# A 3-block transformer kernel: single-unit weight ring, rewritten first norm, respaced top-k, rotations and output-projection waits

## The reference

```python
def rmsnorm(x, g):
    xf = x.astype(jnp.float32)
    y = xf * lax.rsqrt(jnp.mean(jnp.square(xf), axis=-1, keepdims=True) + EPS)
    return (y * g.astype(jnp.float32)).astype(x.dtype)

# block 1, mixer: h = rmsnorm(x); p = h @ w_in, split into the parts of two branches
#  sparse attention: index scores per query block of 128, then
_, idx = lax.top_k(score, n_keep)          # n_keep = 128 keys a query
#  and softmax attention over those keys, 8 heads of 64
#  retention: 4 heads, q and k turned by rotary(), decay mask, group norm, silu gate
return jnp.concatenate([a_out, r_out], axis=-1) @ w_out   # "output projection"

# block 3, first branch: forget-gate attention ("fox")
c = jnp.cumsum(jax.nn.log_sigmoid(f_logit.astype(jnp.float32)), axis=1)
s = s + (ci[..., :, None] - c_t[..., None, :])            # row sums added to the logits
```

## Time and profile before

| what | value |
|---|---|
| median of 3 runs | 2392.09 us |
| the profiled execution's own time | 2387.57 us |
| its span | 2385.8 us |
| granted TensorE clock, mean | 0.999 |
| busy: PE, VectorE, ScalarE, GpSimd | 98%, 46%, 36%, 39% |
| DMA, mean | 87 GB/s |

### The profile page before, as it was taken

How to read it: one execution, slowest core, us unless ns; L and a number is a source line. 1 busy time by engine, 2 the same in 40 slices (tenths; PEclk the granted TensorE clock), 3 DMA queues, 4 the chain that set the end, 5 groups by cost and what they waited for, 6 DMA issues and landing times.

```text
span 2385.8 us, 37842 instructions
## 1 busy us (share of the span) xinstructions
PE 2348.3 (98%) x15316; PEld 2066.7 (87%) x15316; DVE 1103.0 (46%) x1676; ACT 854.6 (36%) x1320; POOL 919.2 (39%) x382
## 2 busy tenths in 40 slices
PE   7999999999999999999999999999999999999999
PEld 7898999999999999898988888767667888888887
DVE  4885353573442534555644435343473337422222
ACT  4334433332222334554322224454464333322222
POOL 4321223344444442123444444422224455444443
PEclk9999999999999999999999999999999999999999
DMA  5121222222222231111232222322213333323232
GB/s 179 66 72 37 73 65 87 89 88 93 87 103 88 88 107 59 54 54 54 89 105 88 90 104 89 107 72 71 71 54 106 106 106 106 106 88 105 88 106 88
DMA packets 33463, 208.12 MB, mean 87 GB/s; under 512 B 3754, under 2 KB 6420, under 8 KB 9284
## 3 DMA queue, kind: packets, MB, share of 16 engines
q1 hardware_dynamic: 29552, 202.00, 24.7%
q10 hardware_dynamic: 3796, 4.45, 0.6%
HBM read 204.24 MB, written 2.12 MB: 86 GB/s over the span
## 4 chain that ended last, share of the span: by engine, by line
issue 59%; POOL 24%; PE 16%; POOLq 1%; DMA 0%; ACT 0%; DVE 0%; SPq 0%; DVEq 0%; ACTq 0%
POOL wl L2574 24%; PE ps L393 14%; PE ps L346 1%; PE ps L328 1%; POOLq L2573 0%; POOLq L2578 0%; DMA raw<-in_w_all 0%; ACT L431 0%; ACT wh L431 0%; PE ps L489 0%; DVE X L464 0%; SPq L2541 0%; DVEq L464 0%; ACTq L430 0%
## 5 line engine op out<-in xcount | busy, mean ns | idle before, releaser
L2574 POOL TENSOR_TENSOR wl<-raw,wh 128x1024 fp32r<-128x1024 f32 x376 | 918.9, 2448 | 1450.0 <-ACT wh L431 1449.8
L431 ACT ACTIVATE wh<-raw 128x1024 fp32r<-128x1024 f32 x376 | 395.2, 1054 | 758.3 <-PE ps L393 501.5
L393 PE MATMUL ps<-Hh,wl 128*128 128x264 f32 (+2 forms) x1736 | 480.6, 325 | 0.0
L393 PE MATMUL ps<-Hl,wh 128*128 128x264 f32 (+2 forms) x1736 | 480.6, 325 | 0.0
L393 PE MATMUL ps<-Hh,wh 128*128 128x264 f32 (+2 forms) x1736 | 480.5, 325 | 0.0
L393 PEld LDWEIGHTS ps<-Hh,wh 128*128 128x128 f32 x1736 | 291.7, 188 | 28.5 <-issue 0.2
L393 PEld LDWEIGHTS ps<-Hh,wl 128*128 128x128 f32 x1736 | 291.1, 188 | 27.8
L393 PEld LDWEIGHTS ps<-Hl,wh 128*128 128x128 f32 x1736 | 291.1, 188 | 27.4
L346 PE MATMUL ps<-Hh,wh 128*128 128x264 f32 (+1 forms) x1056 | 277.4, 326 | 4.9 <-DVE arena L365 4.0
L346 PE MATMUL ps<-Hl,wh 128*128 128x264 f32 (+1 forms) x1056 | 255.9, 306 | 0.0
L346 PE MATMUL ps<-Hh,wl 128*128 128x264 f32 (+1 forms) x1056 | 255.8, 306 | 0.0
(11 more groups left out here) (255 smaller groups left out, 2810.8 us busy)
## 6 DMA issues: line engine op xcount, KB each, us to landing
raw<-in_w_all SPq DMA_DIRECT2D x188, 1024.0 KB, 4.8
X<-in_xT SPq DMA_DIRECT2D x4, 528.0 KB, 9.3
arena<-scratch ACTq DMA_DIRECT2D x2, 1024.0 KB
arena<-in_extra ACTq DMA_DIRECT2D x2, 528.0 KB
out<-X SPq DMA_DIRECT2D x1, 1024.0 KB, 4.2
out<-X SPq DMA_DIRECT2D x4, 256.0 KB, 2.0
arena<-in_extra ACTq DMA_DIRECT2D x2, 264.0 KB
cst<-in_consts SPq DMA_DIRECT2D x1, 448.0 KB, 11.1
```

The lines of the kernel that those rows point to most:

```text
L393: mm = pe.matmul(ps[:, 2 * j + h + bank, 0:c1 - c0], w[:, j, k, :], moving(x, blk, c0, c1), start=(at == 0 and part == 0), stop=(at == len ...
L431: act.activation(wh[:, j], raw[:, j // 2, :, P * (j % 2):P * (j % 2) + P], ACT.Copy).then_inc(hi_split, 1)
L2574: pool.tensor_tensor(wl[:, j], raw[:, j // 2, :, P * (j % 2):P * (j % 2) + P], wh[:, j].bitcast(F32), ALU.subtract).then_inc(split_ready[j ...
```

## The change

Eight edits, in the order of the diff:

- The loads carry one unit each: `raw` has 4 slots of 512 KB with a semaphore each, slot j is loaded again when unit j's own split is ready. `lay_weights` lays the units singly.
- The PE first multiplies zeros: 7 fp32 matmuls of 128x128 by 128x512 (`first_sums`) into PSUM bank 7, after GpSimd has set 512 words of `Yf` to zero. Their result is not used.
- `pe_first` of the first stage takes the first three blocks unit by unit, and the sum of squares goes behind block 6.
- The first norm has its own functions, `first_act` and `first_dve`, with 8 squares instead of a ring of 4. The low parts of units 0 to 3 are made by VectorE (`low`), and GpSimd begins with unit 4. ScalarE loads the table of Sqrt first of all.
- SyncE issues unit 0, X piece 0, unit 1, X piece 1 and so on.
- Top-k in the pair steps: one round a step in steps 0 to 2 and 4 to 15, two in step 3.
- The late rotations move one turn back, the output projection waits bank by bank, and in Fox the selector copies go ahead of the filling and the second packing goes to n = 4, behind the last root.
- At n = 2 of Fox the root goes ahead of the middle part of the rows.

```diff
-        NORM_AT = 5
+        NORM_AT, FIRST_NORM_AT, FIRST_SUMS = 5, 6, 7
...
-        raw = sb("raw", [P, 2, KB, 256])
+        raw = sb("raw", [P, 4, KB, P])
-        raw_landed = [sem(f"raw_landed{s}") for s in range(2)]
+        raw_landed = [sem(f"raw_landed{j}") for j in range(4)]
...
+        def still():
+            return Yf[:, 0:T2]
+
+        def first_sums(pe):
+            pe.wait_ge(pool_zero, 3)
+            for _ in range(FIRST_SUMS):
+                pe.matmul(ps[:, 7, :], still()[:, 0:P], still(), start=True, stop=True)
...
-            for group in [(k, units[:3]) for k in range(KB)] + [(k, units[3:]) for k in range(KB)]:
+            early = 3 if before is not None else 0
+            groups = [(0, units[:1]), (1, units[:1]), (0, units[1:2]), (1, units[1:2]), (2, units[:2]), (0, units[2:3]),
+                      (1, units[2:3]), (2, units[2:3])] if early else []
+            groups += [(k, units[:3]) for k in range(early, KB)] + [(k, units[3:]) for k in range(KB)]
...
-                if k == NORM_AT and len(group[1]) == 3:
+                if k == (FIRST_NORM_AT if early else NORM_AT) and len(group[1]) == 3:
...
+        def first_act(act, gain, first):
...
+            split_hi(act, 0, 16)
+            act.wait_ge(par_landed, 16)
+            block(0), block(1)
+            split_hi(act, 1, 16)
+            square(0), square(1)
+            block(2)
+            split_hi(act, 2, 16)
+            block(3)
+            square(2)
+            block(4)
+            split_hi(act, 3, 16)
+            block(5), square(3), block(6), square(4), block(7)
+            square(5), square(6), square(7)
+            tables_store(act, dsa_views()["tables"])
...
+            rms_std.by(act.activation(cols(rs_view(T1), T1), acc(j, T1), ACT.Sqrt, bias=eps[:, 0:1], scale=1.0 / D))
+
+        def first_dve(v, gain):
...
+            def low(j):
+                v.wait_ge(hi_split, j + 1)
+                v.tensor_tensor(wl[:, j], raw[:, j], wh[:, j].bitcast(F32), ALU.subtract).then_inc(split_ready[j], 1)
...
+            low(0), block(0), block(1)
+            low(1), block(2), add(0)
+            low(2), block(3), add(1), block(4), add(2), block(5), add(3), block(6), block(7)
+            low(3), add(4), add(5), add(6), add(7)
+            rms_std.take(v, "dve")
+            dve.by(v.reciprocal(rs_view(T1), rs_view(T1)))
...
             def between(n):
-                if n < 2:
-                    top_k(3, (11, 13)[n], (13, ROUNDS)[n])
-                elif n < 9:
-                    top_k(4, 2 * n - 4, 2 * n - 2)
+                if n < 3:
+                    top_k(3, 11 + n, 12 + n)
+                elif n < 16:
+                    top_k(4, n - 2 if n > 3 else 0, n - 1)
...
-        ROT_TURN = {0: 2, 2: 3}
+        ROT_TURN = {1: 2, 3: 3}
...
             st = PLAN["b_out"]
-            pe.wait_ge(sig["ret_std"].sem, 4)
-            pe.wait_ge(sig["ret_t"].sem, 8)
-            wait_evacuated(pe, PLAN["b_g1"])
+            free = [(acc_free[(RET_LAST - 1) % 4], (RET_LAST - 1) // 4 + 1), (sig["ret_t"].sem, 7), (sig["ret_t"].sem, 8),
+                    (sig["ret_std"].sem, 4)]
...
                             pe.wait_ge(acc_free[j], u // 4)
+                            pe.wait_ge(*free[b])
...
             sig["row_log"].by(act.activation(d["l"], d["l"], ACT.Ln, bias=1.0))
+            act.wait_ge(tables_landed.sem, TB1 + 16 * len(CONSTS2) + 16)
+            for name in ("selneg", "sele"):
+                ins = act.activation(d[name + "_r"], d[name], ACT.Copy)
+            sig["sel_made"].by(ins)
             fill(8)
...
+                if n:
+                    hn_root(act, n - 1, d["f_rs"], 2, 0, n <= 2)
                 if n == 2:
                     part_mid(act, d, 68)
-                if n:
-                    hn_root(act, n - 1, d["f_rs"], 2, 0, n <= 2)
                 if n == 3:
                     sig["part_lo"].take(act, "act")
                     part_pack(act, d, d["f_parts_r"], 0, 0)
+                if n == 4:
                     part_pack(act, d, d["m_parts_r"], 12, 32)
-                    act.wait_ge(tables_landed.sem, TB1 + 16 * len(CONSTS2) + 16)
-                    for name in ("selneg", "sele"):
-                        ins = act.activation(d[name + "_r"], d[name], ACT.Copy)
-                    sig["sel_made"].by(ins)
...
             sp.dma_start(par[:, :], params).then_inc(par_landed, 16)
-            load(0, 0)
             xs = xT.rearrange("(b p) t -> p b t", p=P)
             for q in range(4):
+                load(q, q)
                 sp.dma_start(X[:, 2 * q:2 * q + 2, :], xs[:, 2 * q:2 * q + 2, :]).then_inc(x_landed[q], 16)
-                if q == 0:
-                    load(1, 1)
             sp.dma_start(cst[:, :], consts).then_inc(cst_landed, 16)
-            with sp.Fori(1, LOADS // 2) as i:
-                for s in range(2):
-                    sp.wait_ge(split_ready[2 * s + 1], i * 1)
-                    load(i * 2 + s, s)
+            with sp.Fori(1, UNITS // 4) as i:
+                for j in range(4):
+                    sp.wait_ge(split_ready[j], i * 1)
+                    load(i * 4 + j, j)
...
-            split_lo(0)
+            pool.memset(still(), 0.0).then_inc(pool_zero, 1)
...
+            first_sums(pe)
             dsa_pe(pe)
...
+            act.preload_act_table(ACT.Sqrt)
             tables_load(act, dsa_views()["tables"])
```

More of the change, by code:

```diff
@@ L321, in pe_first @@
                         pe.wait_ge(split_ready[j], n)
-                        if len(group[1]) == 1:
+                        if group[1] == units[3:]:
                             rms_std.take(pe, "pe")
@@ L339, in pe_first @@
                         pe.wait_ge(acc_free[js], ns - 1)
-                    norm_pe(pe, T, js, both)
+                    norm_pe(pe, T, js, both, first_views() if early else None)
         def three_products(pe, bank, j, k, x, blk, first, last, T=T1):
@@ L496, in norm_act @@
             views = norm_views(T, both)
[L497 to L498 removed]
+            act.preload_act_table_set("natural_log_exp_and_others")
             for b in range(KB):
[L500 to L510 removed]
+                j, n = unit(stage, b % 4, b // 4)
+                if stage is PLAN["b_out"] and b < 4:
+                    act.wait_ge(unit_done[j], n)
+                    split_hi(act, j, (n + 1) * 16)
+                act.wait_ge(acc_free[j], n)
                 x = X[:, b, off:off + T]
                 n_hi.by(act.activation(normed(T)[0][:, b], norm_cols(x, T), ACT.Copy, scale=param(gain, b)))
[L513 removed]
+                if not (stage is PLAN["b_out"] and b < 4):
                     split_hi(act, j, (n + 1) * 16)
@@ L542, in norm_dve @@
             for b in range(KB + 1):
-                if b < KB and stage is not None:
+                if b < KB:
                     residual_unit(v, stage, T, off, b // 4, b % 4)
@@ L570, in norm_dve, with first_views, block, square @@
             rms_std.take(v, "dve")
-            if stage is None:
-                dve.by(v.reciprocal(rs, rs))
-                dve.last(v)
+        def first_views():
+            cut = Cut()
+            return cut(KB * T1, a=KB), cut(T1)
+        def first_act(act, gain, first):
+            squares, _ = first_views()
+            def block(b):
+                act.wait_ge(x_landed[b // 2], 16)
+                n_hi.by(act.activation(normed(T1)[0][:, b], norm_cols(X[:, b, :], T1), ACT.Copy, scale=param(gain, b)))
+            def square(b):
+                sq_made.by(act.activation(squares[:, b], X[:, b, :], ACT.Square))
+            split_hi(act, 0, 16)
[12 more added lines that the diff above has]
+            tables_store(act, dsa_views()["tables"])
+            sq_used.take(act, "act", KB)
+            j, _ = unit(*first)
+            rms_sum.take(act, "act")
+            rms_std.by(act.activation(cols(rs_view(T1), T1), acc(j, T1), ACT.Sqrt, bias=eps[:, 0:1], scale=1.0 / D))
@@ new lines, in first_dve, with block, add @@
+        def first_dve(v, gain):
+            squares, total = first_views()
+            xh, xl = normed(T1)
+            def low(j):
+                v.wait_ge(hi_split, j + 1)
+                v.tensor_tensor(wl[:, j], raw[:, j], wh[:, j].bitcast(F32), ALU.subtract).then_inc(split_ready[j], 1)
+            def block(b):
+                n_hi.take(v, "dve")
+                h_ready.by(v.scalar_tensor_tensor(out=xl[:, b], in0=norm_cols(X[:, b, :], T1), scalar=param(gain, b),
+                                                  in1=xh[:, b].bitcast(F32), op0=ALU.mult, op1=ALU.subtract))
+            def add(b):
+                sq_made.take(v, "dve")
+                if b:
+                    sq_used.last(v)
+                    sq_used.by(v.tensor_tensor(total, total, squares[:, b], ALU.add))
+                else:
+                    sq_used.by(v.tensor_copy(total, squares[:, 0]))
+            low(0), block(0), block(1)
[4 more added lines that the diff above has]
```

(8 more changed lines are left out.)

46 lines of the change are left out of this document (13 added, 33 removed).

## The result

The changed kernel takes 2372.11 us (median of 4, 2371.47 to 2372.31) against 2392.21 us of the kernel before on the same chip (4, 2391.22 to 2392.62): a ratio of 0.9922 with the 95% interval 0.9911 to 0.9934, 20.1 us less. The prediction was faster, 2379.3 us, with a range that ended at 2374.5: the direction was right, and the gain was 7 us larger than forecast. The profiled executions, 2387.57 and 2372.01 us, lie only 15.6 us apart. So the miss has two parts: 2.8 us between the profiles (15.6 against the sum's 12.8), and 4.5 us by which the executions of before lie above its profiled one.

A forecast was written before the change was run, and what follows sets the result against it. The PE was taken as the bound, busy 2348.3 of 2385.8 us. Terms of -5.7 (start), -3.6 (top-k), -1.3 (rotations), -1.0 (output projection) and -1.2 (Fox) sum to -12.8: 2392.1 to 2379.3 us, range 2374.5 to 2386.5.

The forecast's parts named there:

- The step that failed: From profile to timed runs: the median's 4.5 us above the profiled execution was taken to stay after the change.
- The Fox term: Fox gate: splitting six DMA issues around the root lets u_read end earlier, cutting the PE's wait; -1.2 us (-2.1 to 0).
- Top-k: Sparse attention: one round fewer at step 8 frees VectorE earlier, shrinking three evacuation waits of 4.0 us; -3.6 us (-4.3 to -2).
- Start: First three units' groups: earlier data and zeros raising the clock end them at 30.2 us, not 35.9; -5.7 us (-7.3 to -5.0).
- Rival 1: Start: zeros hold the PE without raising the clock, groups end 1.0 us later than before; 2386.0 us, chance 0.10.
- Rotations and output projection: Late rotation number 3 finds number 2 done, -1.3 us; output projection's first unit no longer waits for the last evacuation, -1.0 us.
- The ring: Weight loads of one unit each: twice the issues, loads up to a unit earlier, no PE waits; 0 to -0.5 us.
- Rival 3: Every unit: single loads not overlapping make the weight stream the bound; 2416 us at 5.5 us a load, chance 0.02.
- Rival 2: Start works, but later waits return elsewhere (top-k scaling, rotation, packed rows), the rest giving 0 to -2; about 2385 us, chance 0.12.
- Rival 4: Whole kernel: the PE regains the stretches elsewhere or edits cancel, within 4.8 us of before; about 2390 us, chance 0.04.

The follow-up runs named there:

- busy_waits2: Kernel before, both long waits left, with unread TensorE products added in them (top-k ones in step 10, others in Fox): 2387.47 us, ratio 0.9982.
- start_alone: Kernel before with only the new first norm, zeros, table load and single-unit ring: 2383.61 us, ratio 0.9967.
- no_fox: Changed kernel with the Fox edit undone (selector copies, middle part and second packing back at their old places): 2374.35 us.
- zeros_alone: Kernel before with only the seven products over zeros added ahead of the first block: 2391.95 us, ratio 1.0001.
- no_start: Kernel before with the top-k, late rotation, output projection and Fox edits, without the new start and ring: 2379.24 us, ratio 0.9945.
- ring_busy: Kernel before with single-unit loads in four 512 KB slots, plus unread TensorE products in both long waits: 2386.24 us.
- ring_alone: Kernel before with only the loads changed to single units in four slots of 512 KB: 2388.63 us, ratio 0.9989.
- less_wait: Changed kernel with selector copies further ahead and the second packing behind u_read, to remove two more waits: 2371.29 us, ratio 0.9915.
- fox_alone: Kernel before with only the Fox edit (selector copies, middle part and second packing moved): 2386.82 us, ratio 0.998.
- busy_waits: Kernel before with unread TensorE products added at Fox's wait and in top-k step 8, which had no wait: 2390.42 us, ratio 1.0.
- topk_alone: Kernel before with only the top-k rounds spread one a step: 2385.49 us, ratio 0.9979.

## Why the prediction was right or wrong

- **The step that failed**: "the median of the runs is 2392.09 us, 4.5 us more, which I take to stay". It did not stay: the changed kernel's median, 2372.11 us, is within 0.1 us of its profiled execution. The difference was no fixed cost around the kernel but, for the most part, time at 1.2 GHz behind two waits that the change removes. By the profiles it is a fall at top-k (1.5 us), a longer fall in Fox (1.5) and a later rise at the start (0.5 to 1.7, 1.2 in the middle), 4.2 of the 4.5. busy_waits2 shows the first two by experiment: filling the waits alone gives 4.4 us. The third is read from the profiles of other kernels with the same start. The waits were in the list of the earlier trace rows, and the prediction priced them at their own length.
- **The Fox term** (-1.2) left out the low clock behind the gate, 1.55 us, although it stood in the profile: the 512-column products behind it stepped 0.43 us where they step 0.23. The wait itself gave 1.8 us instead of 1.2 (within -2.1 to 0). In medians Fox was worth 4.3 alone.
- **Top-k** -3.6: the waits gave 3.5, at the size and place predicted (0.6 us left against 0.4). In the median 5.7, with 1.5 of clock and 0.7 that lies in the runs' spread.
- **Start** -5.7: -6.3 at the end of the three units' groups. They end at 29.8 us (30.2 predicted) against 36.1 in the trace of before; the prediction's 35.9 had that end 0.2 early. Two errors met here, and that the sum came out close is partly luck. The zeros end at 9.6 us and not 10.6, and the data comes later than walked: the first Hl ends at 8.7 instead of 7.9 us in this profile and later in others. Six profiles with the changed start and the zeros reach 40 us between 5.2 (start_alone) and 6.7 us (no_fox) ahead of before. In medians the start is worth 5.6 to 6.4 with the later falls kept out. That before's own clock rises later in other executions was the same blind spot again. Rival 1, that the clock does not rise in the zeros, fell: seven of them take 8.0 us in zeros_alone, not 12. That run shows another way to lose them: a gap of 2.26 us behind the zeros, and the clock is low again.
- **Rotations and output projection** -1.3 and -1.0: -1.4 and -1.0 by alignment, and no_start's sum closes with them.
- **The ring** 0 to -0.5: 0.4 to 1.2 us by ring_busy. What the term left out is that the first half of a first load lands earlier (the first block product starts 0.6 us earlier in ring_alone), which was counted only in the start's walk. That it costs nothing held: a load of 512 KB lands in a median of 3.6 us over the whole run, and no wait for a raw load is in TensorE's list.

```profile
raw<-in_w_all SPq DMA_DIRECT2D x376, 512.0 KB, 3.6
```

- The Trainium skill's DMA: Bandwidth & Descriptors asks for batches of 1 MiB or more (under Bandwidth, in its measured table). The measurement decides against it for this kernel: 512 KB a load cost nothing and gained 0.4 to 1.2 us, at a mean of 88 GB/s and with no wait of TensorE for a raw load. **Rival 3** fell with it.
- **Rival 2**, that later waits come back elsewhere, happened at 0.4 us (L794), which less_wait takes away. Rival 4, under 4.8 us in all, fell with the 20.1.
- Together: start 6.3 and its late rise 1.2, top-k 3.5 and its fall 1.5, rotations and output projection 2.4, Fox 1.8 and its fall 1.55 to 3.1, which is 18.3 to 19.8 of 20.1. The sizes are from single profiled executions; what is left lies within the spread of the starts.

## What to carry to other kernels

Where a kernel's executions spread and the profiled one is at the fast end, ask first which of its waits can cost more than their own length; look at the granted clock and at the step of equal matmuls in the few us behind every wait, and price a removed wait with what may follow it. If a wait can't be removed, work that nobody reads may hold the clock: here 1.7 us of it in each of two waits was worth 4.4 us. Added work ahead of the first product paid here only where the real work was ready when it ended.

## What the runs showed that I had not expected

- Behind waits of 2.10 to 2.26 us the clock fell in some executions and stayed in others: of six profiles with the 2.15 us wait at top-k, four show a fall of about 1.5 us (start_alone, fox_alone, ring_alone, zeros_alone), and two none (before and busy_waits). Behind the Fox gate all six profiles with its wait show a fall, of 1.6 us in before and topk_alone and of 3.1 to 3.2 in start_alone, ring_alone, zeros_alone and no_fox. What decides it is open.
- At a cold start the granted clock's column reads 1.00 while equal pairs step 0.44 instead of 0.24 us (before, 12 to 19 us); after the zeros and a 2.26 us gap it reads 0.50 for the same step. The step tells the level in both cases, the column in one.
- The rise at the start varies as well: in five other profiles with the start of before, the first matmul stands within 0.3 us of the same place, and TensorE is 0.5 to 1.7 us behind by 40 us.
